# Feed-forward hidden blocks transposed by VectorE in 32x32 pieces instead of by TensorE

## The reference, cut to what matters

```python
D_MODEL, SEQ, D_FF = 1024, 256, 2816

def swiglu(x, w_gu, w_down):                     # stages of the first block
    g, u = jnp.split(x @ w_gu, 2, axis=-1)
    return (jax.nn.silu(g) * u) @ w_down

def swiglu_ffn(h, w_gate, w_up, w_down):         # stages of the second block
    return (jax.nn.silu(h @ w_gate) * (h @ w_up)) @ w_down

x = x + 0.5 * rms_norm(swiglu(rms_norm(x, g1), w_gu, w_down), g2)    # first block
x = x + 0.5 * swiglu_ffn(rms_norm_2(x, n), w_gate, w_up, w_down)     # second block
```

## Time and profile before

| what | value |
|---|---|
| time, median of 3 runs | 1928.03 us (1926.66 to 1928.61) |
| profiled execution | span 1925.8 us from first to last instruction, 24460 instructions; no whole time is given for it, and the median of the runs stands 2.2 us above the span |
| TensorE busy | 1917.2 us, 100% of the span |
| TensorE weight loads busy | 1599.3 us, 83% |
| VectorE busy | 1200.1 us, 62%, 1872 instructions |
| ScalarE busy | 1101.0 us, 57%, 1892 instructions |
| GpSimd busy | 160.6 us, 8% |
| granted TensorE clock | 9 (the top digit) in all 40 slices |

### The profile page before, as it was taken

One profiled execution on the slowest core, in us unless ns is written; L12 is line 12 of the kernel. 1 busy time (PEld: TensorE's weight loads), 2 busy tenths in 40 slices (PEclk: granted clock), 3 DMA queues, 4 the chain that ended last, 5 costly groups with the idle time before them and its releaser, 6 DMA issues.

```text
span 1925.8 us, 24460 instructions
## 1 busy us (share of the span) xinstructions
PE 1917.2 (100%) x9294; PEld 1599.3 (83%) x9294; DVE 1200.1 (62%) x1872; ACT 1101.0 (57%) x1892; POOL 160.6 (8%) x193
## 2 busy tenths in 40 slices
PE   9999999999999999999999999999999999999999
PEld 7888998888888898888888888888888888888887
DVE  6555787556655668655655567665565555856554
ACT  6555876455655587555655566555455555655543
POOL 1220030000000013000000014100000000600000
PEclk9999999999999999999999999999999999999999
DMA  7665545554665553655466645355556554535553
GB/s 282 209 208 172 190 136 185 194 196 165 206 215 195 175 190 115 229 195 179 152 198 202 208 139 181 116 186 185 185 177 206 192 189 141 183 118 187 186 196 110
DMA packets 97780, 350.22 MB, mean 182 GB/s; under 512 B 10880, under 2 KB 12032, under 8 KB 97408
## 3 DMA queue, kind: packets, MB, share of 16 engines
q1 hardware_dynamic: 95184, 340.13, 52.8%
q10 hardware_dynamic: 2448, 8.53, 1.5%
q0 software_dynamic: 32, 0.00, 0.0%
HBM read 347.57 MB, written 1.05 MB: 181 GB/s over the span
## 4 chain that ended last, share of the span: by engine, by line
PE 93%; DVE 4%; DMA 1%; ACT 1%; issue 1%; SPq 0%; POOL 0%; DVEq 0%; POOLq 0%; ACTq 0%
PE ps_gu L450 17%; PE ps_gu L452 17%; PE ps_gu L451 17%; PE ps_acc L450 10%; PE ps_acc L452 10%; PE ps_acc L451 10%; PE ps_tr L497 2%; PE ps_gu L739 1%; PE ps_gu L741 1%; PE ps_gu L740 1%; DMA sb_raw<-stream 1%; DVE sb_wl L1993 1%; PE ps_acc L470 1%; PE ps_tr L450 0%; PE ps_tr L451 0%
## 5 line engine op out<-in xcount | busy, mean ns | idle before, releaser
L450 PE MATMUL ps_gu<-sb_wh,sb_xh 128*128 128x512 f32 (+2 forms) x1592 | 637.3, 400 | 0.3 <-DVE sb_wl L1990 0.3
L452 PE MATMUL ps_gu<-sb_wh,sb_xl 128*128 128x512 f32 (+2 forms) x1592 | 620.3, 390 | 0.0
L451 PE MATMUL ps_gu<-sb_wl,sb_xh 128*128 128x512 f32 (+2 forms) x1592 | 617.9, 388 | 0.0
L1988 DVE SCALAR_TENSOR_TENSOR sb_wl<-sb_raw,sb_const,sb_wh 128x512 fp32r<-128x512 f32 x346 | 258.7, 748 | 238.4 <-ACT sb_wh L1308 238.1
L1993 DVE TENSOR_TENSOR sb_wl<-sb_raw,sb_wh 128x1024 fp32r<-128x1024 f32 (+2 forms) x294 | 354.5, 1223 | 40.5 <-ACT sb_wh L1311 39.2
L452 PEld LDWEIGHTS ps_gu<-sb_wh,sb_xl 128*128 128x128 f32 x1592 | 298.7, 188 | 62.7
L1311 ACT ACTIVATE sb_wh<-sb_raw 128x1024 fp32r<-128x1024 f32 (+2 forms) x294 | 304.6, 1044 | 79.8 <-DMA sb_raw<-stream 63.0
L451 PEld LDWEIGHTS ps_gu<-sb_wl,sb_xh 128*128 128x128 f32 x1592 | 299.9, 188 | 54.4
L450 PEld LDWEIGHTS ps_gu<-sb_wh,sb_xh 128*128 128x128 f32 x1592 | 299.0, 188 | 55.4 <-issue 1.2
L1307 ACT ACTIVATE sb_wh<-sb_raw,sb_const 128x512 fp32r<-128x512 f32 x346 | 247.5, 715 | 153.8 <-PE ps_acc L452 144.3
L450 PE MATMUL ps_acc<-sb_wh,sb_fr 128*128 128x512 f32 (+1 forms) x768 | 300.0, 391 | 1.8 <-DVE sb_scratch L2513 0.8
(11 more groups left out here) (278 smaller groups left out, 1557.1 us busy)
## 6 DMA issues: line engine op xcount, KB each, us to landing
sb_raw<-stream SPq DMA_DIRECT2D x620, 512.0 KB, 4.4
sb_raw<-stream SPq DMA_DIRECT2D x8, 416.0 KB, 3.8
sb_raw<-stream SPq DMA_DIRECT2D x8, 390.0 KB, 3.6
sb_scratch<-stream SPq DMA_DIRECT2D x6, 512.0 KB, 8.1
sb_gpost<-post_gains ACTq DMA_DIRECT2D x6, 512.0 KB, 6.7
sb_params<-params ACTq DMA_DIRECT2D x2, 1128.5 KB, 8.2
sb_scratch<-gain_rows ACTq DMA_DIRECT2D x4, 512.0 KB, 7.0
sb_raw<-stream SPq DMA_DIRECT2D x4, 384.0 KB, 3.0
```

The costliest lines, as they stand in the source:

```text
L450: pe.matmul(out, xh, wh, start=start, stop=False)
L451: pe.matmul(out, xh, wl, start=False, stop=False)
L452: return pe.matmul(out, xl, wh, start=False, stop=stop)
L1988: stt(m.wl[:, u % RING, 0:512], m.unit(u)[:, 0:512], m.gpre[:, e, k:k + 1], m.wh[:, u % RING, 0:512].bitcast(F32), ALU.mult, ALU.subtract)
```

## The change

- 152 of the 176 hidden blocks are no longer turned by TensorE: those of the chunks 1 to 9, and (0, 1). The blocks (0, 0), (10, 0) and (10, 1) of each stage, which lie in the seams, are still turned by TensorE (`turned_by_tensor`).
- VectorE turns the others (`flip_hidden`). A block is 128 tokens by 256 units, seen as two 128x128 halves. For each of 4x4 pairs of partition groups one transpose instruction reads 32 partitions (tokens) of both halves and writes 32 partitions (units), two 32x32 squares: 16 instructions for each block. The innermost loop keeps the output partitions and moves the input partitions; the outer loop moves the output partitions. The result lies in a new SBUF tile `flip`.
- `flip_hidden` waits for `hidden` of the same block on the same engine, and stands on VectorE before a weight split that comes before `hidden_low`.
- `hidden_high` and `hidden_low` of these blocks read `flip` in SBUF instead of `tr` in PSUM.
- The places for the high and low parts grow from three to four (two chunks of two tiles).
- In `steady` the splits are distributed anew, on both engines: 1 in front of `hidden_low(j, 0)` (ScalarE: in front of `hidden_high(j, 0)`) and 3 behind it, instead of 2 and 2. On VectorE one of the two down units is split before `hidden_low(j-1, 1)` and one behind it.

```diff
@@ places and the new tile @@
-        self.hh = self.fr[:, 0:768].rearrange("p (t n) -> p t n", t=3)
-        self.hl = self.fr[:, 768:1536].rearrange("p (t n) -> p t n", t=3)
+        self.flip = self.carve(3072, 2, CW)
+        self.hh = self.fr[:, 0:1024].rearrange("p (t n) -> p t n", t=4)
+        self.hl = self.fr[:, 1024:2048].rearrange("p (t n) -> p t n", t=4)
...
-    return 2 if t and j == CHUNKS - 1 else t
+    return 2 * (j % 2) + t
+def turned_by_tensor(j, t):
+    return j == LAST or j == 0 and t == 0
@@ TensorE, steady @@
             gate_up(f, j, 0, 1)
-            turn_hidden(f, j - 1, 1)
             gate_up(f, j, 0, 2)
...
             gate_up(f, j, 1, 1)
-            turn_hidden(f, j, 0)
             gate_up(f, j, 1, 2)
@@ TensorE, each seam: turn_hidden(f, LAST - 1, 1) is taken out @@
@@ ScalarE, steady @@
             hidden_high(f, j - 1, 1)
             silu(f, j, 0)
-            split(2)
+            split(1)
             hidden_high(f, j, 0)
-            split(2)
+            split(3)
             silu(f, j, 1)
@@ VectorE @@
+    def flip_hidden(f, j, t):
+        vec.wait_ge(*s.hid_done[t].at(11 * f + j + 1))
+        source = m.hid[:, t, :].rearrange("p (i n) -> p i n", i=2)
+        out = m.flip[:, t, :].rearrange("p (i n) -> p i n", i=2)
+        for a in range(4):
+            for b in range(4):
+                of_units, of_tokens = slice(32 * a, 32 * a + 32), slice(32 * b, 32 * b + 32)
+                v = vec.transpose(out[of_units, :, of_tokens], source[of_tokens, :, of_units])
+        v.then_inc(*s.flipped[t].up())
...
     def steady(f):
         for j in range(1, LAST):
-            split(2)
+            flip_hidden(f, j - 1, 1)
+            split(1)
             hidden_low(f, j - 1, 1)
+            split(1)
             hidden(f, j, 0)
-            split(2)
+            flip_hidden(f, j, 0)
+            split(1)
             hidden_low(f, j, 0)
-            split(2)
+            split(3)
             hidden(f, j, 1)
@@ VectorE, each seam: flip_hidden(f, LAST - 1, 1) is put first @@
```

More of the change, by code:

```diff
@@ L220, in __init__ @@
         self.turned = [Signal(nc, f"hidden_turned_{t}") for t in two]
+        self.flipped = [Signal(nc, f"hidden_flipped_{t}") for t in two]
         self.hid_high = [Signal(nc, f"hidden_high_{t}") for t in two]
@@ L413, in hidden_place, with turn_count @@
 def hidden_place(j, t):
-    return 2 if t and j == CHUNKS - 1 else t
+    return 2 * (j % 2) + t
+def turned_by_tensor(j, t):
+    return j == LAST or j == 0 and t == 0
+def turn_count(f, j, t):
+    kind = turned_by_tensor(j, t)
+    return sum(turned_by_tensor(c, t) == kind for c in range(CHUNKS)) * f + sum(
+        turned_by_tensor(c, t) == kind for c in range(j + 1))
 def by_head(a, n):
@@ L639, in post @@
         gate_up(f, LAST, 0, 2)
-        turn_hidden(f, LAST - 1, 1)
         gate_up(f, LAST, 0, 3)
@@ L1348, in hidden_high @@
     def hidden_high(f, j, t):
-        act.wait_ge(*s.turned[t].at(11 * f + j + 1))
-        go(m.hh[:, hidden_place(j, t), :], m.tr[t][:, 0:CW], ACT.Copy).then_inc(*s.hid_high[t].up())
+        if turned_by_tensor(j, t):
+            act.wait_ge(*s.turned[t].at(turn_count(f, j, t)))
+            source = m.tr[t][:, 0:CW]
+        else:
+            act.wait_ge(*s.flipped[t].at(turn_count(f, j, t)))
+            source = m.flip[:, t, :]
+        go(m.hh[:, hidden_place(j, t), :], source, ACT.Copy).then_inc(*s.hid_high[t].up())
     def load_gain(e):
@@ L2051, in hidden_low @@
         place = hidden_place(j, t)
-        tt(m.hl[:, place, :], m.tr[t][:, 0:CW], m.hh[:, place, :].bitcast(F32), ALU.subtract).then_inc(
+        source = m.tr[t][:, 0:CW] if turned_by_tensor(j, t) else m.flip[:, t, :]
+        tt(m.hl[:, place, :], source, m.hh[:, place, :].bitcast(F32), ALU.subtract).then_inc(
             *s.hid_low[t].up())
@@ L2106, in post @@
     def post(f, e):
+        flip_hidden(f, LAST - 1, 1)
         split(1)
```

## The result

The kernel after takes **1996.07 us** (median of 4 runs, 1995.13 to 1999.89) against 1928.16 us for the kernel before (4 runs, 1926.66 to 1928.61): ratio 1.0357, 95% interval 1.0343 to 1.0372. It is 68 us slower. The forecast was 1958 us: the direction holds and so does the mechanism in the steady chunks, but not at the entry of a stage, and the size is more than twice what I gave it.

The account below looks back on a forecast made before the run. TensorE was taken to set the pace, with VectorE taking over after the change. At c = 0.25: -40 saved, +59 longer chunks, +8 and +3 seams, net +30 on 1925.8, giving 1958 us; range 1888 to 2005.

Parts of the forecast that it names:

- TensorE saves 40: On TensorE, 152 turns removed at 0.26 us each save 40 us.
- c = 0.25, serial: On VectorE, start-to-start time of one transpose, 0.25 us, each waiting for the last; ends kept at 0.14 and 0.31.
- the filling of the square: Reason for serial transposes on VectorE: a square can't be written before all its 32 input columns are in.
- Rival 1: Pipelined transposes on VectorE, 0.13 to 0.20 us apart, so TensorE keeps its gain of 40: 1889 us; chance 30%.
- Rivals 2 and 3: VectorE transposes serial but short (0.20 to 0.236), 1889 to 1926 us, 13%; or dear (0.28 to 0.31), up to 2097, 12%.
- rival 4: TensorE's turns lie in the shadow of something else, so removing them doesn't do what it says; chance next to nothing.
- the sum for c = 0.245: Total time given for transposes 0.245 us apart, estimated from a skill page's 311 ns for 128 bf16 elements: 1943 us.
- VectorE's chunk 9.30 + 32c = 17.30: VectorE's time per steady chunk: 9.30 us of other work plus 32 transposes, 0.98 longer than TensorE's 16.32.
- VectorE is without gaps, ScalarE is hidden, the DMAs cost nothing: In steady chunks VectorE never idles, ScalarE with 8.7 us stays hidden; later weight DMAs cost nothing, up to 5 us.
- 8 + 3: At seams: 8 us for the early `hidden_low(9, 1)` at three seams, 3 us for extra delay in crowded VectorE orders.
- The allowance of 3: At the seams, extra delay in crowded VectorE orders, 0 to 6 us, taken as 3.
- the slack with which the first is met: At each stage's start `hidden_low(j-1, 1)` ends 1.4 us before TensorE wants it, subtracted from 8.8 us of loss per stage.

Follow-up runs that it names:

- e4: Kernel after, but VectorE turns only the 72 blocks (1..9, 0) and TensorE the others; 1913.84 us, ratio 0.9932 to the kernel before.
- e1: Kernel after, but all transposes read input partitions 0 to 31, output partitions changing every fourth time (wrong output); 1893.32 us, ratio 0.9824 to the kernel before.
- e2: As e1, with the two loops exchanged so output partitions change at every transpose (wrong output); 1996.93 us, ratio 1.0359 to the kernel before.
- e3: Kernel after, but TensorE turns all blocks; only the four places and new split order remain; 1930.14 us, ratio 1.0014 to the kernel before.
- e9: As e3, but VectorE turns block (0, 1) of each stage, 8 in all; 1950.51 us, ratio 1.0121 to the kernel before.
- e5: Kernel after, but TensorE also turns block (0, 1) of each stage, leaving VectorE 144 blocks; 1980.37 us, ratio 1.0275 to the kernel before.
- e10: As e4, but with the weight splits in the order of the kernel before; 1942.44 us, ratio 1.0070 to the kernel before.
- e6: Kernel after, but VectorE turns only the 80 t = 1 blocks of chunks 0 to 9; 2029.10 us, ratio 1.0531 to the kernel before.

## Why the prediction was right in kind and wrong in size

- **What bounds the kernel**: right. TensorE was full; every saved turn pays where VectorE keeps up (e4).
- **TensorE saves 40** (152 x 0.26): right. A steady chunk without its two turns lasts 16.32 instead of 16.85 (e1), 0.265 a turn.
- **c = 0.25, serial**: right, 0.251. Of the reasons I gave, the changing partitions hold (e2) and the filling of the square does not (e1). Rival 1, pipelined transposes, falls with it; its time, 1889, was nearly right for its condition (e1: 1893). Rivals 2 and 3 fall with c, rival 4 with e4. One slip of adding: the sum for c = 0.245 comes to 1946 us, not 1943.
- **VectorE's chunk 9.30 + 32c = 17.30**: right, measured 17.33 to 17.34. Over the 64 chunks between first and last `down` of a stage that is 2 us.
- **VectorE is without gaps, ScalarE is hidden, the DMAs cost nothing**: right in nearly all steady chunks. In two of the 72 a late landing cost 1.3 us in all; in the longer, 18.39 us, ScalarE waits 4.27 us for a weight unit. At the stage entry ScalarE is not hidden.
- **The seams, start and end**: 8 + 3 forecast, and 8 x 0.98 of the ninth chunks, which are felt at the first `down` of a seam, less the 2 for their eight turns: 17. Measured 22.3 + 1.4 = 24, so 7 short. The allowance of 3 is about what the new order costs there by itself (e3). Two things were left out. In mix1 two weight splits, not one, stand between the flip and `hidden_low`, and TensorE waits 2.22 us there. And after the long waits in both mix1 and both mix2 seams TensorE's clock falls for a while (last section), some 1.6 us each time.
- **The step that failed: "from it goes the slack with which the first is met: ... `hidden_low(j-1, 1)` ends ... 6.7 after `gate_up`'s end and is wanted ... 8.2 after it, so 1.4."** Between TensorE's marks the forecast was 8 x (8 x 0.98 - 1.4) - 37 (144 turns at 0.26) = +14, and the traces have +45. Of these 31, 2 are the longer chunk and 29 are this term: not 1.4 won at each stage but 2.2 lost.

The term took the flip to start 1.2 us after `gate_up(0, 1)` ends (0.2 + 0.47 + 0.04 + 0.51). In the eight stages it starts 5.6, 5.4, 5.3, 5.3, 4.9, 4.1, 3.9 and 3.6 us after it, 4.8 on average. That is 3.6 us later than assumed, turns +1.4 into -2.2, and makes 8 x 3.6 = 29 us. The entry of the second feed-forward stage in the trace after, ScalarE, VectorE, and TensorE in turn:

```profile
315.81 0.72 ACT L1314 ACTIVATE sb_wh<-sb_raw,sb_const 128x512 fp32r<-128x512 f32 x1 [1.36 <-DMA sb_raw<-stream]
...
317.06 0.45 ACT L1353 ACTIVATE sb_scratch<-ps_gu,sb_stat 128x256 f32<-128x256 f32 x1
```

```profile
317.54 0.48 DVE L2058 SCALAR_TENSOR_TENSOR sb_scratch<-ps_gu,sb_stat,sb_scratch 128x256 f32<-128x256 f32 x1 [1.38 <-ACT sb_scratch L1353]
317.94 0.74 DVE L2000 SCALAR_TENSOR_TENSOR sb_wl<-sb_raw,sb_const,sb_wh 128x512 fp32r<-128x512 f32 x1
318.60 0.75 DVE L2002 SCALAR_TENSOR_TENSOR sb_wl<-sb_raw,sb_const,sb_wh 128x512 fp32r<-128x512 f32 x1
319.27 3.98 DVE L2069 STREAM_TRANSPOSE sb_scratch<-sb_scratch 32x64 f32<-32x64 f32 x16
...
324.42 0.42 DVE L2076 TENSOR_TENSOR sb_fr<-sb_scratch,sb_fr 128x256 fp32r<-128x256 f32 x1
```

```profile
313.87 0.40 PE L464 MATMUL ps_acc<-sb_wh,sb_fr 128*128 128x512 f32 x1
...
324.89 0.79 PE L464 MATMUL ps_acc<-sb_wh,sb_fr 128*128 128x512 f32 x1 [2.68 <-DVE sb_fr L2076]
325.48 0.63 PE L465 MATMUL ps_acc<-sb_wl,sb_fr 128*128 128x512 f32 x1
325.91 0.63 PE L466 MATMUL ps_acc<-sb_wh,sb_fr 128*128 128x512 f32 x1
```

`gate_up(0, 1)` ends where `down` begins, at 313.87. `silu` could follow some 0.2 later, but stands on ScalarE behind a split whose weights have not landed: it starts at 317.06, 3.0 late. One more gate/up unit then stands on VectorE between `hidden` and the flip, 1.33 more (in seven of the eight stages). The other entries differ in detail: in the third and the fifth stage `silu` is only 0.6 late, and this unit itself waits for its weights; in the seventh, without the unit, `hidden` alone is late. The flip starts at 319.27, and TensorE, which has only `down` (2.72) and one `gate_up` (5.44) to do, runs out of work at 322.2. The first waits of the eight stages (the idle time of the row and 0.16 by which the matmul before it outlasts a step) are 3.03, 2.84, 2.73, 2.70, 2.41, 1.61, 1.36 and 1.06: 17.7 us together.

The trace before showed this. The same entry there, on ScalarE, VectorE and TensorE:

```profile
304.65 0.73 ACT L1307 ACTIVATE sb_wh<-sb_raw,sb_const 128x512 fp32r<-128x512 f32 x1 [1.17 <-DMA sb_raw<-stream]
305.28 0.71 ACT L1308 ACTIVATE sb_wh<-sb_raw,sb_const 128x512 fp32r<-128x512 f32 x1
305.89 0.45 ACT L1346 ACTIVATE sb_scratch<-ps_gu,sb_stat 128x256 f32<-128x256 f32 x1
```

```profile
306.38 0.48 DVE L2046 SCALAR_TENSOR_TENSOR sb_scratch<-ps_gu,sb_stat,sb_scratch 128x256 f32<-128x256 f32 x1 [1.37 <-ACT sb_scratch L1346]
306.78 0.74 DVE L1988 SCALAR_TENSOR_TENSOR sb_wl<-sb_raw,sb_const,sb_wh 128x512 fp32r<-128x512 f32 x1
```

```profile
302.71 0.40 PE L450 MATMUL ps_acc<-sb_wh,sb_fr 128*128 128x512 f32 x1
```

`silu` at 305.89 is 3.2 us behind the `down` at 302.71 that follows `gate_up` there too; it cost nothing, as the turn by TensorE after it takes 0.27 and not 4. I put the order of a steady chunk, without stalls, in the place of a row. With 4.8 in place of 1.2 the term would have been -2.2, and the forecast 30 + 29 = 59 above: 1987 us. e9 confirms it by itself (20 us for eight flips over e3).

The 29 us divide in two: 8 x 1.4 = 11 are slack that I had subtracted and that isn't there, and 17.7 are the first waits. e5 bears the second part out: with the entry flip gone it gains 16, which is 17.7 less 2 for eight turns back on TensorE. It does not gain the 11 as well. TensorE sets the pace of the first chunk then, VectorE waits for it, and what it is early doesn't accumulate. I had expected that it would.

## What to carry to other kernels

Before work is moved onto a faster-looking idle engine, price one instruction of it at the start-to-start time, with the start partitions that it will have, and compare the mover's whole chunk with that of the engine relieved: here 17.34 against 16.32, and half of the work moved (e4) pays while all of it costs. Look also at what stands between the moved piece and its user: one weight split more there turned a gain of 14 us into a loss of as much (e10). Then draw the ring of waits through all engines, since an engine with idle time can still be late each time round (e6). Steady-state slack doesn't hold at the entry of a loop: read that place in the trace by itself, row by row.

## What the runs showed of the hardware

- Transposes of 64 elements on 32 partitions start 0.126 us apart when nothing moves and 0.25 when the start partition of the output (e2) or of the input (kernel after) changes, with the same instruction. Their durations are 194 (e1) and 235 ns (e2) in the median, so a duration alone would not have given either figure.
- TensorE comes out of some long waits at the lower of its two clock levels, 1.2 of 2.4 GHz. In the kernel after, behind the wait of 2.68 us, the matmuls start 0.43 us apart from 325.48 to 327.62 instead of 0.227; the seven steps from 324.89 to 327.94 take 3.05 us instead of 1.59, at a granted clock of 0.50 (first row; the second is the same length behind the 0.57 us of waiting at 359.76, at 1.00).

```profile
324.89:327.79 2.90, 2.90 (x7) 2.32 (x8) 2.80 (x8) 0.00 (x0) 0.00 (x0) 0.50 0.69 202
359.76:362.66 2.90, 2.90 (x13) 2.40 (x14) 2.80 (x8) 0.46 (x1) 0.00 (x0) 1.00 0.74 208
```

- The length of the wait does not decide it alone. Of the ten waits of 2.2 us and more in the kernel after, five are followed by the lower level (2.22, 2.68, 2.22, 3.47, 3.47) and five are not (2.87, 2.56, 2.54, 2.25, 3.44).
- What it costs depends on who sets the pace. Behind 324.89 it cost 0.2 us: VectorE sets the pace there, and only its next `hidden` comes a little late, behind a late `gate_up` (a chunk of 17.53 instead of 17.33). The stage's nine chunks (158.3 us) are no longer than those of the first stage (158.4), whose wait of 2.87 left the clock at 1.00. Where TensorE sets the pace it costs some 1.5 us each time. In e9 the step from the first `down(0, 1)` to the next `down` takes 10.07 us in the fifth stage, after a wait of 2.13 and at 0.50 (first row), and 8.55 in the fourth, after a wait of 2.34 and at full rate; the second row is the first stage, behind a wait of 2.89.

```profile
986.58:989.48 2.90, 2.90 (x7) 2.34 (x8) 1.47 (x2) 0.00 (x0) 0.00 (x0) 0.50 0.73 202
32.12:35.02 2.90, 2.90 (x13) 2.41 (x14) 1.48 (x2) 0.47 (x1) 0.98 (x2) 1.00 0.71 202
```

- The seams show it too. The two mix1 seams of e5 both have a wait of 2.23 us; the first, at the lower level, takes 134.5 us between TensorE's marks, the second 132.8. The plain seam takes 40.7 us in e5, at the lower level behind 3.39 us, and 39.1 in the kernel after, at full rate behind 3.44. By these, the four seams of the kernel after that were slowed cost it an estimated 6 us of its 68.
